# Border of the two blocks: turns one weight slot later, the gate's row in its own order, second reciprocal ahead of a low part

## What is computed

```python
        out = merge_branches(z, (y_a, y_b, y_c), w_branch[l], w_out[l])
        x_new = x + gt[:, None] * rms_norm(out, norm_post[l])
...
    for layer in range(DEPTH):
        h = h + FFN_RESIDUAL_WEIGHT * swiglu(rmsnorm(h, ffn1_norm[layer]),
                                             ffn1_w_gate[layer], ffn1_w_up[layer], ffn1_w_down[layer])
```

## Time and profile before

| | us |
|---|---|
| median of 3 runs | 1908.47 |
| lowest, highest | 1906.66, 1908.93 |
| the profiled execution | 1913.72 |
| its span | 1911.6 |
| TensorE busy | 1879.3 (98%) |
| VectorE busy | 1336.3 (70%) |
| ScalarE busy | 1002.5 (52%) |
| mean granted TensorE clock | 0.993 |

### The profile page before, as it was taken

The page is one execution under the profiler, slowest core; times in us unless marked ns, Lnnn a source line. Parts: engine busy times, 40 slices in busy tenths (PEclk is TensorE's granted clock), DMA queues, the critical chain, the costliest instruction groups (busy, mean ns, idle before and its releaser), DMA issues.

```text
span 1911.6 us, 26253 instructions
## 1 busy us (share of the span) xinstructions
PE 1879.3 (98%) x10688; PEld 1589.7 (83%) x10688; DVE 1336.3 (70%) x1826; ACT 1002.5 (52%) x1460; POOL 39.0 (2%) x47
## 2 busy tenths in 40 slices
PE   6999999999999999999999999999999999999998
PEld 2899988999988999988788887788888888778886
DVE  4688888887888888856665566765566555786555
ACT  3455544565544656444554456554455444665444
POOL 1300000000000000000000000000000000000000
PEclk8999999999999999999999999999999999999999
DMA  8544676634676553465467754367765777536775
GB/s 329 198 174 153 233 245 205 198 123 143 239 244 203 204 169 133 146 221 192 155 215 225 230 189 147 131 206 227 223 196 183 227 225 225 170 111 198 223 228 165
DMA packets 123319, 375.17 MB, mean 196 GB/s; under 512 B 14080, under 2 KB 32640, under 8 KB 122432
## 3 DMA queue, kind: packets, MB, share of 16 engines
q1 hardware_dynamic: 118320, 352.11, 56.1%
q0 software_dynamic: 4592, 19.90, 3.1%
q10 hardware_dynamic: 288, 1.51, 0.2%
HBM read 360.87 MB, written 10.49 MB: 194 GB/s over the span
## 4 chain that ended last, share of the span: by engine, by line
PE 90%; DVE 5%; DMA 2%; ACT 2%; issue 1%; SPq 0%; DVEq 0%; ACTq 0%
PE PS L676 27%; PE PS L678 27%; PE PS L677 27%; DMA raw<-weights 2%; DVE w_lo L2108 2%; PE PS L850 1%; PE PS L869 1%; ACT w_hi L1513 1%; PE PS L1092 1%; PE PS L960 1%; PE PS L1259 1%; PE PS L941 1%; DVE arena L2269 1%; PE PS L759 1%; PE PS L1248 1%
## 5 line engine op out<-in xcount | busy, mean ns | idle before, releaser
L2108 DVE TENSOR_TENSOR w_lo<-raw,w_hi 128x1024 fp32r<-128x1024 f32 x600 | 730.0, 1231 | 390.9 <-ACT w_hi L1513 389.6
L1513 ACT ACTIVATE w_hi<-raw 128x1024 fp32r<-128x1024 f32 x600 | 625.2, 1056 | 446.6 <-DMA raw<-weights 443.8
L676 PE MATMUL PS<-w_hi,h_hi 128*128 128x512 f32 (+1 forms) x1280 | 494.8, 387 | 2.1 <-DVE w_lo L2108 1.3
L678 PE MATMUL PS<-w_hi,h_lo 128*128 128x512 f32 (+1 forms) x1280 | 488.4, 382 | 0.0
L677 PE MATMUL PS<-w_lo,h_hi 128*128 128x512 f32 (+1 forms) x1280 | 488.0, 381 | 0.0
L676 PEld LDWEIGHTS PS<-w_hi,h_hi 128*128 128x128 f32 x1280 | 240.7, 188 | 54.5 <-issue 5.1
L678 PEld LDWEIGHTS PS<-w_hi,h_lo 128*128 128x128 f32 x1280 | 240.7, 188 | 47.2
L677 PEld LDWEIGHTS PS<-w_lo,h_hi 128*128 128x128 f32 x1280 | 240.8, 188 | 45.7 <-issue 1.0
L676 PE MATMUL PS<-h_hi,w_hi 128*128 128x256 f32 x896 | 261.4, 292 | 3.0 <-DVE h_lo L2126 2.5
L676 PE MATMUL PS<-w_hi,g_hi 128*128 128x512 f32 (+1 forms) x656 | 257.2, 392 | 0.7 <-DVE w_lo L2108 0.6
L677 PE MATMUL PS<-h_lo,w_hi 128*128 128x256 f32 x896 | 254.5, 284 | 0.0
(11 more groups left out here) (298 smaller groups left out, 1663.6 us busy)
## 6 DMA issues: line engine op xcount, KB each, us to landing
raw<-weights SPq DMA_DIRECT2D x610, 512.0 KB, 3.7
act_mem<-arena SPq DMA_DIRECT2D x144, 64.0 KB, 3.0
arena<-act_mem SPq DMA_DIRECT2D x36, 256.0 KB, 3.8
qk<-weights POOLq DMA_DIRECT2D x12, 512.0 KB, 4.7
v<-weights POOLq DMA_DIRECT2D x12, 512.0 KB, 4.6
x<-weights SPq DMA_DIRECT2D x8, 512.0 KB, 8.0
qk<-cond_in POOLq DMA_DIRECT2D x2, 1024.0 KB, 5.1
arena<-arena SPq DMA_DIRECT2D x32, 64.0 KB, 2.7
```

The source lines that it names most:

```text
L676: pe.matmul(dst, hi, m_hi_, start=first, stop=False, **kw)
L678: return pe.matmul(dst, lo, m_hi_, start=False, stop=last, **kw)
L1513: nc.scalar.activation(w_hi[:, r, :], raw[:, r, :], ACT.Copy).then_inc(w_hi_ready, 1)
L2108: V.tensor_tensor(w_lo[:, r, :], raw[:, r, :], f32(w_hi[:, r, :]), ALU.subtract).then_inc(w_lo_ready, 1)
```

## The change

```diff
-            pool.dma_start(gate_mem.rearrange("o (p k) -> p (o k)", p=P), gate_cols).then_inc(gate_stored, 16)
+            pool.dma_start(gate_mem.rearrange("o (k p) -> p (o k)", p=P), gate_cols, allow_slow_non_contiguous=True).then_inc(gate_stored, 16)
...
-                        if t == 0 and j < len(behind):
+                        if t == 0 and j < len(behind) and behind[j] is not None:
...
-                first_block(start["ffn0"], 0, (0, 1), [lambda: turn_unit(0, 2, OLD_BANKS[2]), lambda: turn_unit(0, 3, OLD_BANKS[3])])
+                first_block(start["ffn0"], 0, (0, 1), [None, lambda: turn_unit(0, 2, OLD_BANKS[2]), lambda: turn_unit(0, 3, OLD_BANKS[3])])
...
-                V.tensor_tensor(scaled_out[:, u, :].rearrange("p (k c) -> p k c", k=4), PS[:, SUM_BANKS[u], :].rearrange("p (k c) -> p k c", k=4),
-                                gate_row.rearrange("p (c k) -> p k c", k=KD)[:, 4 * h:4 * h + 4, :], ALU.mult).then_inc(out_scaled, 1)
+                V.tensor_tensor(scaled_out[:, u, :], PS[:, SUM_BANKS[u], :], gate_row[:, h * BR:(h + 1) * BR], ALU.mult).then_inc(out_scaled, 1)
...
                 low_unit(0, 0)
+                mean_out(1)
                 gain_unit(0, 1, OLD_BANKS[1])
-                mean_out(1)
                 scale_out(3)
                 rstd_out(1)
+                new_unit(2)
                 low_unit(0, 1)
-                new_unit(2)
                 new_unit(3)
+                split(c + 7 + AHEAD)
                 gain_unit(0, 2, OLD_BANKS[2])
-                split(c + 7 + AHEAD)
                 low_unit(0, 2)
```

## The result

| | before | changed |
|---|---|---|
| median, us | 1908.47 | 1915.09 |
| lowest to highest, us | 1906.1 to 1911.29 | 1912.04 to 1918.7 |
| the profiled execution, us | 1913.72 | 1914.41 |
| its span, us | 1911.6 | 1912.3 |

Nine executions of each. The ratio is 1.003, with a 95% interval of 1.0022 to 1.0038: **the change makes the kernel 0.3% slower**, some 5.7 us by the ratio (6.6 between the medians). I had forecast 0.07% faster, and given 5% to what happened.

What follows compares the result with a forecast made beforehand. TensorE was taken as the bound, busy 1879.3 of 1911.6 us. Three border terms (row's order, VectorE's order, turns one slot later) together won 1.35 us, the store costed at nothing, giving 1907.1 us; range 1904.4 to 1909.6.

Steps and rivals of the forecast that it cites:

- The border: Handover from first block's last output sums to second block's first projection; holes of 3.0 us, 1.35 us forecast won.
- the wait before the turn of unit 2: TensorE's wait of 1.53 us for x at the border, before 943.69 us; forecast to vanish with turns one slot later.
- the new wait for slot 2: TensorE's third slot at the border, forecast to idle 1.2 us for VectorE's weight remainder.
- the sum: Second token tile at the border starts at 946.40 instead of 947.75 us: 1.35 us won.
- The store of the gate: Store issued at 822.7 us, now 1024 single values; 1.2 or 12 us on each DMA engine, costed at nothing.
- The slack: At 823 to 845 us, ScalarE's load waits reach 5.11 us before TensorE loses 0.48.
- The rival that happened: Store delays the weights at 823 to 845 us: up to 7 us lost less 1.35, 5.6 slower, 1914.1 us; 5%.
- the row's order: Rival: products with the gate's row stay at 1.13 us despite unit stride; 0.3 us won, 1908.2 us; 6%.
- The gain was not given back: Rival: border's gain is lost later, where VectorE or a load has a fixed time; 1908.5 us; 12%.
- beyond the sum: Rival: all 3.0 us of border holes close if third slot's weights are ready by 943.1; 1905.5 us; 5%.

Runs made afterwards that it cites:

- the orders: New orders of TensorE and VectorE alone, gate's store and strided row as before, against the changed kernel: 1909.47 us, ratio 0.9998 to the kernel before.
- the gate's part: Kernel before with only the store of 1024 single values and the unit-stride row product changed: 1913.06 us against 1909.43, ratio 1.0017.
- SyncE's run: Changed kernel with the store of 1024 single values issued by SyncE among the weight loads, not by GpSimd: 1913.91 us, ratio 1.0022 to the kernel before.

## Why the prediction was wrong

*The border* was right, step by step. The products went from 1134 to 684 ns (0.68 was taken), the wait before the turn of unit 2 went, the new wait for slot 2 came (0.98 idle, 1.2 forecast) and the sum was 1.38 against 1.35. Each part alone is worth less: the orders 0.16, the gate's part 11.85 - 10.9 = 0.9.

*The store of the gate* is the step that failed: "Being of a few bytes they are nearest to the first, so 1.2 us in which a weight load is a little late", costed at nothing. Measured, the store took 11.5 us to land, a weight load beside it 13.5, and TensorE lost 5.0 us to the wait and some 2 to the clock. My two ends were 1.2 and 12 us, from 0.019 and 0.19 us a piece, and I took the lower one. As a price of the packets it was fair: where they can be counted, 1024 of them take 0.7 us on each engine. The step that failed is the one from there to the cost: I took the time of its packets for the time in which the store hinders the loads, and the engines moved nothing or little for some 10 us after these packets. The upper end was near the measured length by luck: it multiplies a time by the number of pieces, and 128 pieces take nearly as long as 1024.

*The slack* of some 5 us before TensorE loses was about right: the load took 10.2 us longer than the 3.3 of the one ahead of it, and TensorE lost 5.0. What my price left out is the clock, which fell during that wait and took about 2 us more.

*The rival that happened* is the store's, at the place and by the mechanism that it named: 5.6 us slower by its working, about 5.7 by the runs. That the two agree so well is luck in part: it priced the wait at 7 us, where 5.0 was measured, and the clock at nothing, where it was 2. What I had wrong is its chance of 5%. Between two ends ten times apart, with nothing to choose by but one row of packets that were larger and fewer, it should have had a third or so, and the range should have reached to it. The rule of the Trainium skill's page "DMA: Bandwidth & Descriptors" ("Rules for kernel authors", one descriptor per element) that I set against this part was cited and then not given weight. The trace agrees with it where the pieces are counted, 1054 packets under 512 bytes in SyncE's run; it gives no time for them.

*The other rivals*: the row's order did save 0.45 us a product, so that rival is refuted. The gain was not given back behind the border: no wait of TensorE behind 950 us was longer than 0.7 in the changed kernel. Nothing beyond the sum was won.

## What to carry to other kernels

A tiny transfer on a shared set of DMA engines is priced by how long the other transfers stand still beside it, not by its bytes and not by the time of its packets; if the trace has no transfer of its shape, keep the upper bound inside the range, or measure it alone. Do not let many partitions write single words side by side in DRAM: store contiguous pieces, and bring them into order on the chip on an idle engine, or leave a gap between them (64 bytes were enough here). Ask of a transfer that may be long where the stream beside it has slack: the same store cost 5 to 7 us of TensorE's time at 818 us and none at 754.

## What the runs showed of the hardware that I had not expected

Single words from different partitions that are neighbours in DRAM take 8.4 to 11.5 us to land, for 128 of them or 1024, and by GpSimd's queue as by SyncE's; 64 bytes between them bring it to 4.2 (by GpSimd's). While such a store is under way, and some 2 us beyond, the weight loads of another queue stand still too: 0 GB/s for 3.5 us and 40 GB/s for 7.5 more. The packets do not show it. From GpSimd's queue the store of 1024 single values has 32 packets, as many as the one before; from SyncE's each value is a packet, and all are through in 0.9 us, some 7 us before the store lands.
